# Accumulators opened earlier, and a few unused matmuls in the gaps of a routing chain

## The chip, the cores and the metric

The program runs on one core of a Trainium2 chip. The metric is the device time of one execution in microseconds, the median of the runs of each kernel. Lower is better.

## What is computed

One block of a streaming encoder for 256 tokens of width 1024, in float32. The first part is a mix of three branches; the second is a mixture of experts:

```
h = rms_norm(x); proj = h @ w_in
x = x + (gated sum of chunk attention, Mamba-2 scan, memory attention) @ w_out
# MoE on rms_norm(x):
logits = xt @ w_router + b_router            # 256 x 32
top_val, top_idx = top_k(logits, 4); wts = softmax(top_val)
for each expert e, for its tokens:
    g = min(x @ w_gate[e] + b_gate[e], 7); u = clip(x @ w_up[e] + b_up[e], -7, 7)
    y += wt * (((u + 1) * g * sigmoid(1.702 * g)) @ w_down[e] + b_down[e])
```

## The kernel before

The 256 tokens are two tiles of 128 (t = 0 and 1). Everything before the experts follows one list of steps, written out by a planner, that each engine walks in the same order. Its last block is `wo`, the product with `w_out`, in column halves i = 0 and 1. Of the last half only tile 0 stands in the list; tile 1 is done by hand, by `second_tile(0)` to `second_tile(3)`, four quarters of six matmuls each (float32r, 512 columns, L1382 to L1384).

Behind that comes the routing chain, in which TensorE, VectorE and ScalarE hand to one another. Per tile t:

- `add_out(t)` (VectorE, L1211) adds the product to the residual `x_sb`; `turn_out(t)` (TensorE transposes, L1369) and `take_xT(t)` (VectorE, L1217) make the transposed copy `xT`;
- `last_logits(t)` (TensorE, L1389, 32 columns) makes the second half of the router's logits. It needs `take_xT(t)`. VectorE finds the norm of the row meanwhile with ScalarE's help (L862 to L874);
- `choose(t)` (VectorE, L1231 to L1241) takes the logits, finds the top four and writes the 0/1 matrix `chosen_r`;
- a matmul with `upto_r` (L1620 for tile 0, L1623 and L1634 for tile 1) counts the place of each token within its expert, and `find_first(t)` (VectorE, L1248, L1250) turns it into `hot`, the selection matrix of expert 0;
- ScalarE writes the normed rows `h2` (L821), and `gather` (TensorE, L1605, 64 columns per instruction) picks the tokens of expert 0 by `hot`.

`take_gathered` (VectorE, L1262) copies the gathered tokens to `xgT`, and the loop over 32 experts begins. Expert 0 runs its gate product first (L1674). Its matmuls are of 512 columns on half of the array, 8 for each load. After the first load's 8 matmuls comes the bias (L1683), which waits for `pick` (VectorE, L1317). VectorE reaches that line only behind the tables of places and weights (L1287 to L1303) and the reading of the number of passes.

Between the logits of tile 1 and the first gather, TensorE opens the four accumulator banks `ACC` = 0 to 3 (L1627): for each one a matmul of one column of zeros with the identity, which marks the bank so that the later scatter products can add to it. They need only that `add_out(1)` has read the last product out of its bank (`gemm_taken`).

The weights of the experts come by SyncE's DMA queue (L457): six loads of 2 MB per expert into eight slots. The first eight are asked for before the loop. Each further one waits until TensorE has used its slot (`e_used`), in the order of the slots: load 8 waits for the first 8 matmuls of expert 0, load 12 for the first half of its down product (L1712).

An instruction of this program that reads float32 (not float32r) stands in the trace as two records.

Of the kernel before, what the change touches and what calls it, by code (L numbers as in the profile page):

```python
# [5 lines left out]
P = 128  # L6
# [14 lines left out]
NB = 512  # L21
# [55 lines left out]
GEMM_AT = {g: n for n, g in enumerate(GEMM)}  # L77
# [3 lines left out]
def first(name, i=0):  # L81

    return QUARTERS * BLOCK_AT[(name, i)]
# [106 lines left out]
def misc_index():  # L190

    at, n = {}, 0
    for step in SCHED:
        at[step] = n
        n += MISC_GROUPS.get(step[0], 0)
        if step[0] == "ssm":
            n += 1 + step[3]
    at["tail"] = n
    at["places"] = n + TT
    at["end"] = n + 2 * TT  # L200
    return at


MISC_AT = misc_index()
# [11 lines left out]
def hybrid_block_kernel(nc, x, mem, g_mix, w_in, w_dt, a_gains, rel_rev, conv_w, conv_b, dt_bias, a_log, d_skip,  # L216
                        g_ssm, g_mem, w_mem_kv, x_gains, w_br_a, w_br_b, w_br_c, w_out, norm_ffn, w_router,
                        b_router, w_gate, b_gate, w_up, b_up, w_down, b_down, bias_dram, out):
    with ExitStack() as ctx:
        def sb(name, shape, dt=F32):  # L220
            return ctx.enter_context(nc.sbuf_tensor(name, shape, dt))
# [3 lines left out]
        def sem(name):  # L225
            if name not in sems:
                sems[name] = ctx.enter_context(nc.semaphore(name))
            return sems[name]
# [11 lines left out]
        def placed(name, shape, dt, offset):  # L240
            return nc.alloc_sbuf_tensor_at(name, shape, dt, offset=base + 4 * offset)
# [3 lines left out]
        SR = placed("regions_r", [P, N_REGIONS, REGION], F32R, 0)  # L245
# [53 lines left out]
        ident = sb("ident", [P, P])  # L299
        upto = sb("upto", [P, P])  # L300
        after = sb("after", [P, P])
# [41 lines left out]
        upto_r = sb("upto_r", [P, P], F32R)  # L343
# [31 lines left out]
        ps = ctx.enter_context(nc.psum_tensor("ps", [P, 8, NB], F32))  # L375
        GEMM_BANKS, EXP_BANK, MISC_BANKS = (0, 1, 2, 3), 7, (4, 5, 6)
        ACC, G_BANK, U_BANK, X_BANK, D_BANK = (0, 1, 2, 3), 4, 5, 6, 7

        gemm_taken = sem("gemm_taken")
# [15 lines left out]
            return (r * LOADS + k) % SLOTS, (r * LOADS + k) // SLOTS  # L395

        MISC_END = MISC_AT["end"]
        COUNT_BANK = EXP_BANK
        GEMM_END = len(GEMM)

        def pool_rests(n):
# [3 lines left out]
        def quarter(w):  # L405

            m = w // 2
            return halves[:, m % HALVES, 2 * (w % 2):2 * (w % 2) + 2], splits[:, w % SPLITS, 0], splits[:, w % SPLITS, 1]
# [432 lines left out]
        def _(dve):  # L841
# [437 lines left out]
            dve.wait_ge(sem("counts_ready"), 1)  # L1279
            dve.tensor_reduce(cmax, ps[:, COUNT_BANK, 0:EXPERTS], AX, ALU.max).then_inc(sem("counts_taken"), 1)  # L1280
            dve.wait_ge(sem("counts_taken"), 1)
# [70 lines left out]
        def _(pe):  # L1352
            misc = [0]

            def group():

                n = misc[0]
                misc[0] += 1
                if n >= 3:
                    pe.wait_ge(misc_taken, n - 2)  # L1360
                return MISC_BANKS[n % 3]
# [6 lines left out]
            def turn(dst, src):  # L1368
                return pe.transpose(dst, src, ident[:])  # L1369
# [10 lines left out]
            def three_passes(out, lhs, rhs, start, stop):  # L1380

                pe.matmul(out, lhs[0], rhs[0], start=start, stop=False, skip_group_check=True)  # L1382
                pe.matmul(out, lhs[1], rhs[0], start=False, stop=False, skip_group_check=True)  # L1383
                return pe.matmul(out, lhs[0], rhs[1], start=False, stop=stop, skip_group_check=True)  # L1384

            def router(t, half):

                for c in range(4 * half, 4 * half + 4):
                    last = pe.matmul(ps[:, EXP_BANK, t * EXPERTS:(t + 1) * EXPERTS], xT[:, c, t * P:(t + 1) * P],  # L1389
                                     wr_sb[:, c], start=(c == 0 and t == 0), stop=(c == KC - 1), skip_group_check=True)  # L1390
                return last

            pe.wait_ge(sem("masks"), 3)
            n = 0
            for step in SCHED:
# [145 lines left out]
                elif kind == "ssm":  # L1541
                    u, g, t = step[1:]
                    if t == 1:
                        b = group()
                        pe.matmul(ps[:, b, :], cbm[:, g % 2, 2 * P:3 * P], fx[:, g * GW:(g + 1) * GW],
                                  start=True, stop=True).then_inc(misc_ready, 1)
# [3 lines left out]
                    for r in range(8):  # L1550
# [3 lines left out]
                                         start=True, stop=True)  # L1554
# [22 lines left out]
            def second_tile(q):  # L1577

                w = first("wo", 1) + q
                hi, lo = quarter(w)[1:]  # L1580
                b = GEMM_BANKS[GEMM_AT[("wo", 1, 1)] % 4]
                for c in range(2):
                    k = 2 * q + c
                    last = three_passes(ps[:, b, :], (mergedT[0][:, k, P:T], mergedT[1][:, k, P:T]),
                                        (hi[:, c], lo[:, c]), k == 0, k == KC - 1)
                last.then_inc(unit_used, 1)

            def turn_out(t):

                b = group()  # L1590
                pe.wait_ge(gemm_taken, GEMM_AT[("wo", 1, t)] + 1)
                for c in range(4):
                    last = turn(ps[:, b, c * P:(c + 1) * P], x_sb[:, t, (4 + c) * P:(5 + c) * P])
                last.then_inc(misc_ready, 1)

            def last_logits(t):

                pe.wait_ge(misc_taken, MISC_AT["tail"] + t + 1)
                router(t, 1).then_inc(sem("logits_ready"), 1)

            def gather(t0=0, t1=TT):

                for t in range(t0, t1):
                    for c in range(KC):
                        last = pe.matmul(ps[:, X_BANK, c * BLK:(c + 1) * BLK], h2[:, t, c * P:(c + 1) * P], hot[:, t],  # L1605
                                         start=(t == 0 and c == 0), stop=(t == TT - 1), skip_group_check=True)
                if t1 == TT:
                    last.then_inc(sem("gather_ready"), 1)

            second_tile(0)  # L1610
            turn_out(0)
            second_tile(1)
            last_logits(0)
            second_tile(2)
            second_tile(3)
            turn_out(1)

            b = group()
            pe.wait_ge(sem("chosen_ready"), 1)
            pe.matmul(ps[:, b, 0:EXPERTS], upto_r[:], chosen_r[:, 0], start=True, stop=True).then_inc(misc_ready, 1)  # L1620
            last_logits(1)
            b = group()
            pe.matmul(ps[:, b, 0:EXPERTS], ones_r[:], chosen_r[:, 0], start=True, stop=False, skip_group_check=True)  # L1623

            pe.wait_ge(gemm_taken, GEMM_END)
            for bank in ACC:
                pe.matmul(ps[:, bank, 0:1], ident[:], after[:, P - 1:P], start=True, stop=False, skip_group_check=True)  # L1627

            pe.wait_ge(sem("hot_ready"), 1)
            pe.wait_ge(sem("h2_ready"), 2)  # L1630
            pe.wait_ge(misc_taken, MISC_AT["places"] + 1)
            gather(0, 1)
            pe.wait_ge(sem("chosen_ready"), 2)
            pe.matmul(ps[:, b, 0:EXPERTS], upto_r[:], chosen_r[:, 1], start=False, stop=True, skip_group_check=True)\  # L1634
                .then_inc(misc_ready, 1)
            pe.wait_ge(sem("logits_taken"), TT)
            for t in range(TT):
                last = pe.matmul(ps[:, COUNT_BANK, 0:EXPERTS], ones_r[:], chosen_r[:, t], start=(t == 0), stop=(t == 1))
            last.then_inc(sem("counts_ready"), 1)
            pe.wait_ge(sem("hot_ready"), 2)  # L1640
            pe.wait_ge(sem("h2_ready"), 4)
            gather(1, 2)

            def scatter(n, signal=None):

                pe.wait_ge(sem("yb_ready"), n + 1)
                for t in range(TT):
                    for h in range(2):
                        rows = slice(64 * h, 64 * h + 64)
                        last = pe.matmul(ps[:, ACC[2 * t + h], :], hot_wT[rows, t], yb[rows], start=False, stop=False,  # L1650
                                         skip_group_check=True)
                        if signal is not None:
                            last.then_inc(signal, 1)
# [8 lines left out]
            with pe.Fori(0, n_pass) as b_:  # L1662
                with pe.Fori(0, EXPERTS // ROUND) as j_:
                    j = b_ * (EXPERTS // ROUND) + j_
                    for r in range(ROUND):
# [3 lines left out]
                        for k in range(4):  # L1669
                            bank, (slot, turns) = (G_BANK, U_BANK)[k // 2], place(r, k)  # L1670
                            pe.wait_ge(e_landed[slot], (j * TURNS + turns + 1) * 16)
                            for c in range(KC // 2):
                                for h in range(2):
                                    last = pe.matmul(ps[64 * h:64 * h + 64, bank, :], xgT[:, k % 2 * 4 + c],  # L1674
                                                     eslots[slot][:, c, h * NB:(h + 1) * NB],
                                                     start=(k % 2 == 0 and c == 0), stop=(k % 2 == 1 and c == 3),
                                                     skip_group_check=True)
                            last.then_inc(e_used[slot], 1)
                            if k % 2 == 0:

                                pe.wait_ge(sem("pick_ready"), i + 1)
                                for h in range(2):
                                    pe.matmul(ps[64 * h:64 * h + 64, bank, :], pick[0:96],  # L1683
                                              bias_parts[0:96, k // 2, h * NB:(h + 1) * NB],
                                              start=False, stop=False, skip_group_check=True)
# [17 lines left out]
                        for h in range(2):  # L1703
                            pe.matmul(ps[64 * h:64 * h + 64, D_BANK, :], pick[0:96],
                                      bias_parts[0:96, 2, h * NB:(h + 1) * NB],
                                      start=True, stop=False, skip_group_check=True)
                        for k in range(2):
                            slot, turns = place(r, 4 + k)
                            pe.wait_ge(e_landed[slot], (j * TURNS + turns + 1) * 16)
                            for c in range(4):  # L1710
                                for h in range(2):
                                    last = pe.matmul(ps[64 * h:64 * h + 64, D_BANK, :], actT[:, c, 64 * k:64 * k + 64],  # L1712
                                                     eslots[slot][:, c, h * NB:(h + 1) * NB],
                                                     start=False, stop=(k == 1 and c == 3), skip_group_check=True)
# [42 lines left out]
```

## Time and profile before

| | us |
|---|---|
| median of three runs | 1543.1 (1540.38 to 1544.27) |
| the profiled execution's own time | 1546.29 |
| its span, from first to last instruction | 1544.3 |
| TensorE busy (matmuls) | 1460.4 |
| VectorE busy | 619.2 |
| ScalarE busy | 391.3 |
| mean granted TensorE clock | 0.984 |

The profiled execution is 3.2 us longer than the median of the runs and 2.0 us longer than the longest of them. Its own time is 2.0 us more than its span. All places in it are counted in microseconds from its first instruction. The routing chain lies at about 597 to 617 us, and the loop over the experts from 617 us to 1538 us.

### The profile page before, as it was taken

How to read it: one execution, taken by the hardware profiler on the slowest of the kernel's cores; microseconds unless marked ns; L12 is line 12 of the kernel's file. 1: busy time of each engine (PE TensorE's matmuls, PEld its weight loads, DVE VectorE, ACT ScalarE, POOL GpSimd, SP SyncE). 2: the span in 40 equal slices, each digit the busy share in tenths (PEclk: the TensorE clock that was granted, in tenths of full speed). 3: DMA queues.
4: the chain of work that ended last, by engine and by line, in shares of the span. 5: the costliest groups of instructions: out<-in, count | busy, mean ns of one | idle time of the engine just before them, and what ended most of it. 6: DMA issues, size and time to landing. Idle time of an engine off the chain costs nothing.

```text
span 1544.3 us, 18679 instructions
## 1 busy us (share of the span) xinstructions
PE 1460.4 (95%) x7595; PEld 849.2 (55%) x7595; DVE 619.2 (40%) x1118; ACT 391.3 (25%) x570; POOL 151.7 (10%) x91
## 2 busy tenths in 40 slices
PE   6978997899999999999999999999999999999998
PEld 6876776777778877444444443433433433443343
DVE  5896569777775585212122221211211111112112
ACT  5435455545545443010010100100100100100010
POOL 4245322111111220000000000000000000000000
PEclk9999999999999997999999999999999999999999
DMA  7334334445444685899999999999999999999996
GB/s 243 114 132 150 104 115 136 144 154 163 144 146 177 237 323 220 334 428 427 429 428 429 429 428 428 429 429 428 428 429 429 429 428 428 429 429 428 428 429 265
DMA packets 72651, 491.39 MB, mean 318 GB/s; under 512 B 5168, under 2 KB 7344, under 8 KB 48032
## 3 DMA queue, kind: packets, MB, share of 16 engines
q1 hardware_dynamic: 69648, 487.76, 78.1%
q10 hardware_dynamic: 2448, 2.62, 0.6%
q0 software_dynamic: 512, 0.43, 0.1%
q8 instruction: 27, 0.44, 0.1%
q14 instruction: 16, 0.13, 0.0%
HBM read 489.72 MB, written 1.07 MB: 318 GB/s over the span
## 4 chain that ended last, share of the span: by engine, by line
PE 63%; DMA 23%; DVE 9%; ACT 2%; issue 2%; POOL 1%; DVEq 0%; SPq 0%; ACTq 0%
DMA regions<-in_w_up 22%; PE ps L1674 18%; PE ps L1712 10%; PE ps L1382 6%; PE ps L1383 6%; PE ps L1384 6%; PE ps L1605 5%; PE ps L1369 3%; PE ps L1650 3%; DVE splits L931 1%; DVE regions L1034 1%; DVE regions L1032 1%; ACT splits L673 1%; PE ps L1540 1%; DVE regions L950 1%
## 5 line engine op out<-in xcount | busy, mean ns | idle before, releaser
L1674 PE MATMUL ps<-regions,sig 128*64 128x512 f32 x2048 | 463.4, 597 | 25.9 <-DMA regions<-in_w_up 25.0
L1674 PEld LDWEIGHTS ps<-regions,sig 128*64 128x64 f32 x2048 | 142.1, 137 | 322.2 <-issue 263.1
L1382 PE MATMUL ps<-splits,regions_r 128*128 128x512 f32 x512 | 215.4, 421 | 11.9 <-DVE splits L931 9.2
L1712 PE MATMUL ps<-regions,tmp 128*64 128x512 f32 x1024 | 225.1, 592 | 0.0
L1383 PE MATMUL ps<-splits,regions_r 128*128 128x512 f32 x512 | 202.7, 396 | 0.0
L1384 PE MATMUL ps<-splits,regions_r 128*128 128x512 f32 x512 | 202.6, 396 | 0.0
L673 ACT ACTIVATE splits<-halves 128x1024 fp32r<-128x1024 f32 x152 | 158.7, 1054 | 107.4 <-PE ps L1384 96.9
L931 DVE TENSOR_TENSOR splits<-halves,splits 128x1024 fp32r<-128x1024 f32 x114 | 142.3, 1256 | 69.9 <-ACT splits L673 69.2
L831 ACT ACTIVATE work<-work 128x512 f32<-128x512 f32 x32 | 20.2, 630 | 528.3 <-DVE work L1327 528.3
L1712 PEld LDWEIGHTS ps<-regions,tmp 128*64 128x64 f32 x1024 | 71.9, 137 | 131.8 <-issue 129.4
L580 POOL TENSOR_TENSOR splits<-halves,splits 128x1024 fp32r<-128x1024 f32 x38 | 93.2, 2451 | 424.0 <-ACT splits L673 424.0
L1605 PE MATMUL ps<-craw,regions 128*128 128x64 f32 x1056 | 125.2, 278 | 0.1
L1605 PEld LDWEIGHTS ps<-craw,regions 128*128 128x128 f32 x1056 | 123.9, 196 | 0.3 <-DVE craw L1250 0.3
L1382 PEld LDWEIGHTS ps<-splits,regions_r 128*128 128x128 f32 x512 | 98.2, 192 | 40.5 <-DVE splits L931 11.9
L1383 PEld LDWEIGHTS ps<-splits,regions_r 128*128 128x128 f32 x512 | 98.1, 192 | 23.0 <-issue 4.1
L1384 PEld LDWEIGHTS ps<-splits,regions_r 128*128 128x128 f32 x512 | 97.9, 191 | 21.7
L1341 DVE COPY sig<-ps 128x512 f32<-128x512 f32 x32 | 22.1, 692 | 208.9 <-PE ps L1712 208.9
L1332 DVE TENSOR_SCALAR work<-ps 128x512 f32<-128x512 f32 x32 | 22.1, 692 | 193.7 <-PE ps L1674 193.7
L1327 DVE TENSOR_SCALAR work<-ps 128x512 f32<-128x512 f32 x32 | 22.1, 692 | 173.3 <-PE ps L1674 173.3
L833 ACT ACTIVATE craw<-ps 128x256 f32<-128x256 f32 x32 | 12.3, 383 | 289.7 <-PE ps L1369 289.7
L1262 DVE TENSOR_TENSOR sig<-ps,gain_rows 128x512 f32<-128x512 f32 x33 | 22.8, 691 | 144.6 <-PE ps L1605 144.6
L1650 PE MATMUL ps<-sig,craw 64*128 64x512 f32 x264 | 65.6, 615 | 0.8 <-DVE sig L1341 0.8
(243 smaller groups left out, 1346.4 us busy)
## 6 DMA issues: line engine op xcount, KB each, us to landing
regions<-in_w_gate SPq DMA_DIRECT2D x64, 2048.0 KB, 30.1
regions<-in_w_up SPq DMA_DIRECT2D x64, 2048.0 KB, 33.2
regions<-in_w_down SPq DMA_DIRECT2D x64, 2048.0 KB, 35.4
halves<-in_w_in SPq DMA_DIRECT2D x48, 1024.0 KB, 5.2
halves<-in_w_br_b SPq DMA_DIRECT2D x8, 1024.0 KB, 5.1
halves<-in_w_mem_kv SPq DMA_DIRECT2D x8, 1024.0 KB, 5.1
halves<-in_w_br_a SPq DMA_DIRECT2D x4, 1024.0 KB, 5.1
halves<-in_w_br_c SPq DMA_DIRECT2D x4, 1024.0 KB, 6.9
```

What stands on the lines that cost most here:

```text
L580: pool.tensor_tensor(lo, raw, hi.bitcast(F32), ALU.subtract).then_inc(lo_ready_pool, 1)
L673: act.activation(hi, raw, ACT.Copy).then_inc(hi_ready, 1)
L931: dve.tensor_tensor(lo, raw, hi.bitcast(F32), ALU.subtract).then_inc(lo_ready, 1)
L1262: dve.tensor_tensor(xgT, ps[:, X_BANK, :].rearrange("p (c j) -> p c j", c=KC), gain2_rows[:].unsqueeze(2).to_broadcast([P, KC, BLK]), ALU. ...
L1369: return pe.transpose(dst, src, ident[:])
L1382: pe.matmul(out, lhs[0], rhs[0], start=start, stop=False, skip_group_check=True)
L1383: pe.matmul(out, lhs[1], rhs[0], start=False, stop=False, skip_group_check=True)
L1384: return pe.matmul(out, lhs[0], rhs[1], start=False, stop=stop, skip_group_check=True)
L1605: last = pe.matmul(ps[:, X_BANK, c * BLK:(c + 1) * BLK], h2[:, t, c * P:(c + 1) * P], hot[:, t], start=(t == 0 and c == 0), stop=(t == TT ...
L1650: last = pe.matmul(ps[:, ACC[2 * t + h], :], hot_wT[rows, t], yb[rows], start=False, stop=False, skip_group_check=True)
L1674: last = pe.matmul(ps[64 * h:64 * h + 64, bank, :], xgT[:, k % 2 * 4 + c], eslots[slot][:, c, h * NB:(h + 1) * NB], start=(k % 2 == 0 and ...
L1712: last = pe.matmul(ps[64 * h:64 * h + 64, D_BANK, :], actT[:, c, 64 * k:64 * k + 64], eslots[slot][:, c, h * NB:(h + 1) * NB], start=False ...
```

## The change

Three things change, all on TensorE. The opening of the accumulators moves from behind the logits of tile 1 to ahead of them, with the wait for `gemm_taken` that goes with it. A new helper `keep_busy(bank, n)` issues n matmuls of 512 columns (float32r, operands that lie there anyway) whose result nothing reads. It is called three times: 3 matmuls ahead of `turn_out(1)`, into the bank that the first product of `wo` had; 3 behind the gather of tile 0; and 2 behind the gather of tile 1. The last two calls write to `SPARE_BANK`, the bank that held the places of tile 0.

```
-        COUNT_BANK = EXP_BANK
+        COUNT_BANK, SPARE_BANK = EXP_BANK, MISC_BANKS[MISC_AT["places"] % 3]
...
+            def keep_busy(bank, n):
+
+                for _ in range(n):
+                    pe.matmul(ps[:, bank, :], upto_r[:], SR[:, 2, 0:NB], start=True, stop=True)
...
             second_tile(3)
+            keep_busy(GEMM_BANKS[GEMM_AT[("wo", 0, 0)] % 4], 3)
             turn_out(1)
 
             b = group()
             pe.wait_ge(sem("chosen_ready"), 1)
             pe.matmul(ps[:, b, 0:EXPERTS], upto_r[:], chosen_r[:, 0], start=True, stop=True).then_inc(misc_ready, 1)
+            pe.wait_ge(gemm_taken, GEMM_END)
+            for bank in ACC:
+                pe.matmul(ps[:, bank, 0:1], ident[:], after[:, P - 1:P], start=True, stop=False, skip_group_check=True)
             last_logits(1)
             b = group()
             pe.matmul(ps[:, b, 0:EXPERTS], ones_r[:], chosen_r[:, 0], start=True, stop=False, skip_group_check=True)
-
-            pe.wait_ge(gemm_taken, GEMM_END)
-            for bank in ACC:
-                pe.matmul(ps[:, bank, 0:1], ident[:], after[:, P - 1:P], start=True, stop=False, skip_group_check=True)
...
             gather(0, 1)
+            keep_busy(SPARE_BANK, 3)
             pe.wait_ge(sem("chosen_ready"), 2)
             pe.matmul(ps[:, b, 0:EXPERTS], upto_r[:], chosen_r[:, 1], start=False, stop=True, skip_group_check=True)\
                 .then_inc(misc_ready, 1)
...
             gather(1, 2)
+            keep_busy(SPARE_BANK, 2)
```

## Rows read from the trace of the kernel before

**Rows 1.** The page: the span, and the granted clock in 40 slices (tenths).

```profile
span 1544.3 us, 18679 instructions
...
PEclk9999999999999997999999999999999999999999
```

**Rows 2.** Busy time by stretch: us; PE, PEld, DVE, ACT, POOL; clock, DMA share, GB/s.

```profile
616.00:624.00 8.00, 7.12 (x23) 2.20 (x24) 4.64 (x22) 0.00 (x0) 0.00 (x0) 0.62 0.00 0
624.00:644.00 20.00, 20.00 (x114) 9.47 (x112) 3.85 (x5) 2.89 (x4) 0.00 (x0) 1.00 1.00 410
644.00:646.00 2.00, 2.00 (x12) 0.69 (x10) 0.00 (x0) 0.00 (x0) 0.00 (x0) 1.00 0.72 197
646.00:900.00 254.00, 254.00 (x1362) 109.32 (x1360) 51.02 (x105) 26.03 (x36) 0.00 (x0) 1.00 1.01 428
```

**Rows 3.** What TensorE waited for, 900 to 1544: us in total, times, longest.

```profile
PE ps L1674 <- DMA regions<-in_w_up: 25.0, 39, 1.0
```

**Rows 4.** The chain that ended last, 601 to 630: start, us, what.

```profile
604.68 1.61 PE ps L1389 x8
...
606.48 1.69 PE ps L1627 x8
608.16 3.52 PE ps L1605 x16
...
612.39 3.69 PE ps L1605 x16
...
616.10 0.70 DVE sig L1262
...
616.94 6.20 PE ps L1674 x16
```

**Rows 5.** Busy time by stretch around the routing chain, columns as in rows 2.

```profile
602.00:605.00 3.00, 1.36 (x10) 0.90 (x8) 1.72 (x5) 0.81 (x3) 0.00 (x0) 1.00 0.73 218
605.00:608.00 3.00, 3.00 (x16) 3.00 (x16) 2.38 (x13) 1.96 (x3) 0.00 (x0) 0.51 0.97 371
...
636.00:640.00 4.00, 4.00 (x38) 3.98 (x36) 0.00 (x0) 2.26 (x3) 0.00 (x0) 1.00 0.98 418
```

**Rows 6.** TensorE in order of time: start, us, instruction, [idle before it, its releaser].

```profile
598.61 0.98 PE L1389 MATMUL ps<-wr_sb,regions 128*128 128x32 f32 x8
599.42 0.48 PE L1382 MATMUL ps<-splits,regions_r 128*128 128x512 f32 x1
...
603.27 0.63 PE L1369 MATMUL ps<-ident,regions 128*128 128x128 f32 x4 [0.87 <-DVE regions L1211]
...
604.68 1.61 PE L1389 MATMUL ps<-wr_sb,regions 128*128 128x32 f32 x8 [0.77 <-DVE regions L1217]
...
630.28 3.60 PE L1674 MATMUL ps<-regions,sig 128*64 128x512 f32 x16
...
636.44 3.68 PE L1605 MATMUL ps<-craw,regions 128*128 128x64 f32 x32
```

**Rows 7.** VectorE in order of time.

```profile
606.40 0.25 DVE L1231 SCALAR_TENSOR_TENSOR rt<-ps,stat,head_rows 128x32 f32<-128x32 f32 x1 [0.27 <-PE ps L1389]
...
611.85 0.19 DVE L1248 TENSOR_TENSOR rt<-ps,chosen_r 128x32 f32<-128x32 f32 x1 [3.65 <-PE ps L1634]
...
621.36 0.19 DVE L1317 CAST pick<-cbm 96x64 bf16 x1 [1.50 <-issue]
```

**Rows 8.** ScalarE in order of time.

```profile
606.16 2.30 ACT L821 ACTIVATE regions<-regions,stat 128x512 f32<-128x512 f32 x2 [1.04 <-DVE stat L874]
```

**Rows 9.** Other falls and returns of the clock: stretches as in rows 2, TensorE as in rows 6.

```profile
252.00:256.00 4.00, 0.77 (x4) 0.57 (x4) 3.96 (x4) 4.00 (x7) 0.14 (x1) 1.00 0.00 0
578.00:580.00 2.00, 0.19 (x2) 0.00 (x0) 2.00 (x4) 1.82 (x3) 0.00 (x0) 1.00 0.61 262
...
581.00:584.00 3.00, 3.00 (x9) 2.34 (x8) 1.91 (x3) 0.00 (x0) 0.00 (x0) 0.52 0.02 5
...
458.39 3.55 PE L1369 MATMUL ps<-ident,regions 128*128 128x128 f32 x16 [2.53 <-DVE regions L950]
```

More of the change, by code:

```diff
@@ L397, in hybrid_block_kernel @@
         MISC_END = MISC_AT["end"]
-        COUNT_BANK = EXP_BANK
+        COUNT_BANK, SPARE_BANK = EXP_BANK, MISC_BANKS[MISC_AT["places"] % 3]
         GEMM_END = len(GEMM)
@@ L1608, in gather, with keep_busy @@
                     last.then_inc(sem("gather_ready"), 1)
+            def keep_busy(bank, n):
+                for _ in range(n):
+                    pe.matmul(ps[:, bank, :], upto_r[:], SR[:, 2, 0:NB], start=True, stop=True)
             second_tile(0)
@@ L1615, in _ @@
             second_tile(3)
+            keep_busy(GEMM_BANKS[GEMM_AT[("wo", 0, 0)] % 4], 3)
             turn_out(1)
@@ L1620, in _ @@
             pe.matmul(ps[:, b, 0:EXPERTS], upto_r[:], chosen_r[:, 0], start=True, stop=True).then_inc(misc_ready, 1)
+            pe.wait_ge(gemm_taken, GEMM_END)
+            for bank in ACC:
+                pe.matmul(ps[:, bank, 0:1], ident[:], after[:, P - 1:P], start=True, stop=False, skip_group_check=True)
             last_logits(1)
@@ L1623, in _ @@
             pe.matmul(ps[:, b, 0:EXPERTS], ones_r[:], chosen_r[:, 0], start=True, stop=False, skip_group_check=True)
-            pe.wait_ge(gemm_taken, GEMM_END)
-            for bank in ACC:
-                pe.matmul(ps[:, bank, 0:1], ident[:], after[:, P - 1:P], start=True, stop=False, skip_group_check=True)
             pe.wait_ge(sem("hot_ready"), 1)
@@ L1632, in _ @@
             gather(0, 1)
+            keep_busy(SPARE_BANK, 3)
             pe.wait_ge(sem("chosen_ready"), 2)
@@ L1642, in _ @@
             gather(1, 2)
+            keep_busy(SPARE_BANK, 2)
             def scatter(n, signal=None):
```

## The prediction

> **What bounds the kernel now.** I read the page first: the span is 1544.3 us and the granted clock is full in nearly every slice, so no general slowness of TensorE is at stake [rows 1]. The stretches come next. The reader is to see that from 646 us on the DMA engines are never free (share 1.01, 428 GB/s), that TensorE has no idle time at first, and that it later waits for weights 39 times, 25.0 us in all [rows 2, 3]. The loop over the experts is thus bound by its loads, and its end moves only if the stream of loads starts earlier. It stands still from 616 to 624 us, because all eight slots are full and none is used, and it dips once more at 644 to 646 us, when load 12 waits for its slot [rows 2]. Both dips end when TensorE lets go of a slot. So whatever brings expert 0 forward brings the end forward by as much, provided it still holds at the second dip.
>
> The chain of 601 to 630 us says what expert 0 waits for: almost only TensorE's own instructions [rows 4]. The clock says why they take long. It falls at about 605 us and stays at half (0.50, which is 1.2 GHz of 2.4) until about 622 us [rows 2, 5]. What came before it fell is in the order of time: TensorE was idle 0.87 us for `add_out(1)`, then 0.77 us for `take_xT(1)` [rows 6], busy 1.36 of 3.00 us [rows 5]. At half clock the same router matmuls take 1.61 us instead of 0.98, and 16 gather records take 3.52 us, the time of 32 at full clock [rows 4, 6].
>
> **The change part by part.** Prices at full clock: the eight router records of 598.61 hold TensorE 0.81 us, until 599.42 [rows 6]. A record of 512 columns holds it 0.23 us: 16 of L1674 take 3.60 us, tail included [rows 6]. At half clock it is 0.43: 16 of them take 6.20 us, of which the last 0.9 was at full clock again [rows 2, 4]. I take the same for the unused ones. A gather of one tile is half of 3.68 us less its tail, 1.76 us.
>
> *Three unused matmuls ahead of `turn_out(1)`.* They take 3 x 0.23 = 0.69 us. They start when the last product is issued, 0.87 us before the transposes are released, so they cost nothing [rows 6]. If that cover were gone, or the clock low (3 x 0.43 = 1.3 us), they would push the transposes, `take_xT(1)` and the logits by 0 to 0.4 us.
>
> *The opening of the accumulators.* Eight records; at half clock they are 1.69 us of the chain [rows 4]. At full clock I take the router's 0.81 us, as both load a full set of weights and stream little. The trace has no such record at full clock. The bounds are a clean halving of the 1.69 us, 0.85, were it all clock, and the 1.69 us undivided, were it none; the router's pair of rows, 1.61 and 0.98, says that it is nearly all clock [rows 4, 6]. They go into the gap of 0.77 us ahead of 604.68. The wait for `gemm_taken` that moves with them holds nothing back, since the transposes ahead of it waited for the same release by `add_out(1)`. Behind it stand the logits, which could start up to 0.1 us later. That is covered, because VectorE waits for the logits only until 606.40 and its own norm is ready 0.27 us before that [rows 7].
>
> *The router and `choose(1)`.* The logits end at 604.68 + 0.81 = 605.5. VectorE's norm is then the later one, so L1231 starts at 606.15 instead of 606.40 and `chosen_r` is there at 607.9 [rows 7].
>
> *Gather of tile 0 and three more unused matmuls.* From 605.6 to 607.4, then 0.69 us to 608.1. `chosen_r` is ready at 607.9, so 0.2 us of this lies on the path. L1634, L1248 and L1250 take 0.85 us as now (611.44 to 612.3, of which 0.1 is clock) and lead to 608.95. The rows of `h2` are ready at 606.16 + 2.30 = 608.46, not later [rows 8].
>
> *Gather of tile 1.* 608.95 + 1.76 = 610.7, against 612.39 + 3.69 = 616.08 now. L1262 ends at 611.6 and L1674 starts at 611.75, against 616.94 [rows 4]: 5.2 us earlier. The last two unused matmuls (0.46 us) lie beside L1262, which takes 0.70 us.
>
> *Expert 0.* The first 16 records of L1674 take 3.45 us at full clock instead of 6.03 [rows 4, 6], another 2.6 us. That makes 7.8. But now something else is late. `pick` is written 4.76 us after the end of L1262 (616.79 to 621.55), and no part of that is TensorE's clock [rows 7]. So the bias matmuls, at 622.97 now, can start at 611.6 + 4.76 = 616.4 and not at 615.2. The gain is 7.8 - 1.2 = 6.5 us. The first slot comes free at 615.2, when the eight loads have just landed, and the stream goes on almost without a break; load 12 still finds its slot in use. The second dip moves with TensorE, by 6.5 us [rows 2].
>
> **What the sum rests on** is that the clock holds. For it: the added 0.69 us and the opening fill the two gaps, and a gather at full clock kept it at 1.00 at 636 to 640 us with no matmul of 512 columns in most of it [rows 5]. Against it: the opening streams one column per matmul and may be worth no more than idleness, and a gap alone does not decide. TensorE was busy 0.77 of 4 us at 252 us and the clock stayed at 1.00, but it fell behind the shorter gap at 578 us [rows 9]. Which places are risky depends on where the gate's moments of decision lie.
>
> The Trainium skill, "TensorE: Matmul & The Clock Gate", section "What's actually happening", says that these moments run free of the kernel and meet it elsewhere in each run. The trace agrees in so far as the two gaps above were judged differently; by that rule the second rival below holds in many executions. The same page, section "Part 4: PE-mode transpose", says that transposes do not count as activity. The trace disagrees: the clock went back to full after 458.39 to 461.7 us, in which TensorE did nothing but transposes [rows 9]. By the page the transposes at 603.27 would be another gap, and the clock would more likely fall.
>
> **Against the medians.** The sum is made against the profiled execution, 1546.29 us, and gives 1539.8. That execution is 3.2 us above the median of the runs. If the excess is the clock's (it fell later in the others), the time is that of a held clock in all, 1539.8 or somewhat less; if it is only the profiler's, it is 1543.1 - 6.5 = 1536.6. I take the middle, 1538.2.
>
> **The rivals.**
>
> 1. *The clock holds through the chain* (as summed): 1538.2, own range 1536.0 to 1540.5. Chance 0.45.
>
> 2. *The clock falls after all, a little later, at 605.6 to 607.8 us, in most executions.* The stretch from the unused matmuls' end at 602.9 holds only transposes, the opening, the logits and the start of a gather. Worked through for a fall at 605.6: gather 3.5 us to 609.1, three unused matmuls at 0.43 to 610.4, 1.0 to 611.4, gather to 614.9, L1674 from 616.0, with the clock back somewhat before its end, to 621. For one at 607.8: L1674 from 613.8, end 619.4. Against 622.97 that is 2 to 3.6 us, but an execution of the kernel before with the same late fall has part of that already. Time 1541.2, range 1539.3 to 1543. Chance 0.33.
>
> 3. *The change does not do what it says:* the clock falls at 605 as before. Then the opening at full clock in the gap saves its 1.69 us, and the second group of unused matmuls costs 3 x 0.43 = 1.3 us on the path, as `chosen_r` is long ready by then. The last group, 0.85 us, just fits beside L1262 and its hand-over. Gain 0.4 us: 1542.7, range 1541.5 to 1544. Chance 0.15.
>
> 4. *Slower.* The clock falls before the opening, which then takes 1.69 us in a gap of 0.77, and its return moves from 622 us to later, so that more of expert 0 runs at half clock. Each 16 records there cost 2.6 us more [rows 4, 6]. The opening and the unused matmuls cost 0.9 + 1.3 - 1.69 = 0.5 us net; with two groups of 16 more, 5.7 us: 1548.8. It decides from a return more than about 5 us later. Nothing in the trace holds the clock down while L1674 runs dense that long. Chance 0.07.
>
> **How the numbers follow.** A measurement of this kernel tells about 0.3%, 4.6 us, from no change. The first case passes it in about three of four ways of comparing it, the second hardly ever: faster 0.34 + 0.04 = 0.38. The third, most of the second and the rest of the first are within: 0.56. Slower 0.06. The range runs from the first case's low end, a little widened for its unknown place against the median, to the third case: 1535.5 to 1543.8.
>
> **What the profile after would show.** TensorE's granted clock at 605 to 611 us: 1.00 in case 1, a fall at 605.6 or later in case 2. L1627 between 603.7 and 604.6 with the logits still at 604.7. L1231 at about 606.15. The second gather at 609, L1262 at 611, and behind the first 16 records of L1674 an idle time of about 1.2 us that VectorE's `pick` ends, which is not there now. The DMA engines busy again by 617. The prediction is wrong if the clock holds and the end does not move, which would mean that the loads were not the bound, or if the clock falls in spite of the 0.69 us ahead of the transposes.

## The result, and the profile after

The changed kernel takes 1535.47 us (median of six executions, 1533.17 to 1538.3), the kernel before 1542.39 us (six, 1540.2 to 1549.71). The ratio is 0.995, with a 95% interval of 0.9933 to 0.9967. It is faster, and in this set by more than the 0.3% that the prediction took as the bound of measurement. The prediction was wrong by its range: 1535.47 lies 0.03 us below the low end of 1535.5, and most of its chance stood on no difference.

The page of the profile after, the lines that answer to [rows 1]:

```profile
span 1535.4 us, 18695 instructions
...
PEclk9999999999999999999999999999999999999999
```

The one weaker slice of [rows 1] is gone. Stretches of the changed kernel around the chain, columns as in [rows 2]:

```profile
597.00:600.00 3.00, 2.82 (x18) 2.17 (x16) 1.18 (x3) 1.52 (x3) 0.00 (x0) 1.00 0.88 284
600.00:603.00 3.00, 3.00 (x29) 3.00 (x28) 2.65 (x15) 1.15 (x2) 0.00 (x0) 1.00 0.83 339
603.00:606.00 3.00, 2.65 (x22) 2.42 (x20) 1.88 (x10) 2.87 (x4) 0.00 (x0) 1.00 1.03 434
...
610.00:612.00 2.00, 1.45 (x8) 0.29 (x4) 0.73 (x8) 0.00 (x0) 0.00 (x0) 1.00 0.12 49
612.00:613.00 1.00, 0.52 (x4) 0.31 (x6) 0.76 (x4) 0.00 (x0) 0.00 (x0) 1.00 0.84 164
```

The granted clock is 1.00 all through, where [rows 5] has 0.51. The loads stand still for little more than the 2 us from 610 to 612, where [rows 2] has eight. The chain that ended last, 600 to 630 us, against [rows 4]:

```profile
600.69 0.96 PE ps L1389 x8
601.65 0.10 PE ps L1632
601.75 1.83 PE ps L1605 x16
603.58 0.75 PE ps L1613 x3
...
604.38 0.20 DVE rt L1248
604.61 0.27 DVE craw L1250
...
604.92 2.01 PE ps L1605 x16
606.96 0.69 DVE sig L1262
```

In this kernel L1613 is `keep_busy`, L1629 the opening, L1681 the product of L1674 before, and L1690 its bias. TensorE in order of time:

```profile
598.13 0.86 PE L1613 MATMUL ps<-regions_r,upto_r 128*128 128x512 f32 x3
599.16 0.63 PE L1369 MATMUL ps<-ident,regions 128*128 128x128 f32 x4 [0.18 <-DVE regions L1211]
...
599.66 1.03 PE L1629 MATMUL ps<-after,ident 128*128 128x1 f32 x8
600.58 1.08 PE L1389 MATMUL ps<-wr_sb,regions 128*128 128x32 f32 x8
...
607.80 3.65 PE L1681 MATMUL ps<-regions,sig 128*64 128x512 f32 x16 [0.36 <-DVE sig L1262]
612.49 0.41 PE L1690 MATMUL ps<-bias_parts,pick 96*64 96x512 bf16 x2 [1.03 <-DVE pick L1317]
```

The wait of 0.87 us ahead of the transposes is 0.18 us of idleness now, and the wait ahead of the logits is filled by the opening. Behind the first 16 records of the gate product stands the new wait for `pick`.

The first bias matmul of the kernel before, to compare with the last line:

```profile
622.97 0.39 PE L1683 MATMUL ps<-bias_parts,pick 96*64 96x512 bf16 x2
```

From the first logits record of tile 1 to the first bias matmul of expert 0 the kernel before took 622.97 - 604.68 = 18.29 us, the changed one 612.49 - 600.58 = 11.91 us. The gain of the chain is 6.4 us.

Two other things lie between these executions. The changed kernel comes to its logits 4.1 us earlier (600.58 against 604.68), in code that is the same. And the end is only about 9 us earlier (span 1535.4 against 1544.3), though the first bias is 10.5 us earlier.

### The profile page after: what moved, and what is told of

It reads as the page before. It is cut to its first block, busy times and chain, and to the rows that moved or that the text cites. A ratio compares the mean times of both kernels' runs of the same rounds, so it can differ in the third digit from the quotient of the medians.

```text
span 1535.4 us, 18695 instructions
## 1 busy us (share of the span) xinstructions
PE 1450.0 (94%) x7603; PEld 840.8 (55%) x7603; DVE 618.8 (40%) x1118; ACT 391.0 (25%) x570; POOL 152.8 (10%) x91
## 4 chain that ended last, share of the span: by engine, by line
PE 62%; DMA 23%; DVE 9%; ACT 2%; issue 2%; POOL 1%; DVEq 0%; ACTq 0%
DMA regions<-in_w_up 22%; PE ps L1681 17%; PE ps L1719 10%; PE ps L1382 6%; PE ps L1384 6%; PE ps L1383 6%; PE ps L1605 5%; PE ps L1657 3%; PE ps L1369 3%; DVE regions L1034 2%; DVE splits L931 2%; DVE regions L1032 1%; ACT splits L673 1%; PE ps L1540 1%; DVE regions L950 1%
## 5 line engine op out<-in xcount | busy, mean ns | idle before, releaser
L1681 PE MATMUL ps<-regions,sig 128*64 128x512 f32 x2048 | 461.1, 594 | 26.4 <-DMA regions<-in_w_up 26.1
L1681 PEld LDWEIGHTS ps<-regions,sig 128*64 128x64 f32 x2048 | 141.3, 137 | 321.4 <-issue 259.7
L1382 PE MATMUL ps<-splits,regions_r 128*128 128x512 f32 x512 | 213.6, 417 | 11.8 <-DVE splits L931 9.2
L1605 PE MATMUL ps<-craw,regions 128*128 128x64 f32 x1056 | 121.8, 273 | 0.4 <-DVE craw L1250 0.4
L1605 PEld LDWEIGHTS ps<-craw,regions 128*128 128x128 f32 x1056 | 120.6, 192 | 0.5 <-DVE craw L1250 0.5
L1382 PEld LDWEIGHTS ps<-splits,regions_r 128*128 128x128 f32 x512 | 97.2, 190 | 39.9 <-DVE splits L931 11.7
L833 ACT ACTIVATE craw<-ps 128x256 f32<-128x256 f32 x32 | 12.3, 383 | 291.2 <-PE ps L1369 291.2
```

## The experiments

Each kernel was run 7 to 12 times, and the kernel before 23 to 35 times on the same chip; ratios are to it. One execution of each was profiled, so what is said of a trace is said of one execution. "The chain" is the time from the first logits record of tile 1 to the first bias matmul of expert 0, in the profiled execution.

**The parts alone.** The first four kernels each leave out a part of the change. In the first, only the opening is moved:

```diff
-            keep_busy(GEMM_BANKS[GEMM_AT[("wo", 0, 0)] % 4], 3)
...
-            keep_busy(SPARE_BANK, 3)
...
-            keep_busy(SPARE_BANK, 2)
```

> Only the opening of the accumulators is moved; there are no unused matmuls. Theory A (the change's gain is the clock, which the unused matmuls hold at full through the routing chain): the clock falls in the chain as before, so the chain from the router's last matmuls to the bias of expert 0 keeps most of its half-clock time. The gain is what the eight opening records leave of their 1.69 us on the chain plus what a later fall gives, 1.5 to 2.6 us (ratio 0.998 to 0.999). Rival B (the moved opening is what matters, and the unused matmuls are idle decoration): about the full 6.9 us of the change, ratio 0.9955.

Measured: 1538.63 us, ratio 0.9981 (0.9967 to 0.9996); chain 15.75 us (604.74 to 620.49). Stretches of its profile:

```profile
603.00:605.00 2.00, 1.68 (x16) 1.71 (x16) 1.15 (x5) 0.76 (x3) 0.00 (x0) 1.00 0.84 205
605.00:609.00 4.00, 4.00 (x24) 4.00 (x23) 2.63 (x15) 2.94 (x4) 0.00 (x0) 0.57 0.99 412
609.00:619.00 10.00, 8.98 (x32) 5.81 (x34) 4.63 (x23) 2.33 (x3) 0.00 (x0) 0.50 0.52 220
```

The clock falls at 605.5 and comes back at 619.2 us. The gain of the chain is 2.5 us, within what theory A gave. Rival B, which wanted a ratio of about 0.9955, is out: it lies below the interval.

The second kernel keeps the unused matmuls, with the opening at its old place:

```diff
-            pe.wait_ge(gemm_taken, GEMM_END)
-            for bank in ACC:
-                pe.matmul(ps[:, bank, 0:1], ident[:], after[:, P - 1:P], start=True, stop=False, skip_group_check=True)
             last_logits(1)
             b = group()
             pe.matmul(ps[:, b, 0:EXPERTS], ones_r[:], chosen_r[:, 0], start=True, stop=False, skip_group_check=True)
+            pe.wait_ge(gemm_taken, GEMM_END)
+            for bank in ACC:
+                pe.matmul(ps[:, bank, 0:1], ident[:], after[:, P - 1:P], start=True, stop=False, skip_group_check=True)
```

> The three calls of unused matmuls stay, the opening of the accumulators is back behind the logits. Theory A: the clock holds past 605 us in most executions, but the opening is 0.85 us more on the path at full clock and is one more thin stretch, so the clock may fall at about 608 us: gain 0.6 to 5.8 us. If the clock holds throughout, the loss against the whole change is 0.85 us less the time in which the places of tile 0 are waited for anyway, so a ratio of 0.996 to 0.9965. Rival B: ratio 1.000 or above.

Measured: 1539.46 us, ratio 0.9991 (0.9976 to 1.0006), no difference that can be told, and less than theory A had for a clock that holds; chain 15.70 us (599.07 to 614.77), in the part of the expectation in which the clock falls after all. In its trace the fall has moved to 603.1, 4.0 us behind its first logits record (599.07), where before it was 0.4 us behind:

```profile
599.00:603.00 4.00, 3.94 (x34) 3.94 (x35) 2.93 (x18) 2.64 (x4) 0.00 (x0) 1.00 1.00 414
603.00:606.00 3.00, 2.85 (x12) 2.50 (x12) 1.11 (x6) 1.38 (x2) 0.00 (x0) 0.52 1.00 423
```

The first group of unused matmuls gets the clock past the first danger, and with the opening on the path behind the logits there is a second one. The opening does two things there: it is thin work itself, and it puts the second group later (3.70 us behind the first logits record, against 2.81 in the changed kernel). Which of the two counts is not shown.

The third keeps the moved opening and the first group only:

```diff
             gather(0, 1)
-            keep_busy(SPARE_BANK, 3)
...
             gather(1, 2)
-            keep_busy(SPARE_BANK, 2)
```

> The opening is moved and only the three unused matmuls ahead of the transposes of tile 1 stay. Theory A with all three groups needed: the clock gets past 605 us but falls between the two gathers or behind them, at about 608 us; gain 2 to 3.5 us (ratio 0.998). If the first group alone holds the clock, the gain is that of the whole change plus the 0.2 us that the second group lies on the path, ratio 0.9955, and the later two groups do nothing. Rival B: as the whole change.

Measured: 1537.61 us, ratio 0.9979 (0.9962 to 0.9996); chain 14.98 us (604.25 to 619.23). The clock falls at 608.5 us, 4.2 us behind the first logits record (604.25):

```profile
604.00:608.00 4.00, 3.74 (x32) 3.53 (x31) 3.28 (x19) 2.47 (x3) 0.00 (x0) 1.00 0.96 397
608.00:612.00 4.00, 3.65 (x17) 3.44 (x16) 0.91 (x6) 2.82 (x4) 0.00 (x0) 0.56 1.03 436
```

In the changed kernel the second group runs from 2.8 us behind the first logits record and the third from 6.2 us behind it. At this fall only the second is missing. Whether the third is needed too was not tried.

The fourth has the later two groups only:

```diff
             second_tile(3)
-            keep_busy(GEMM_BANKS[GEMM_AT[("wo", 0, 0)] % 4], 3)
             turn_out(1)
```

> The opening is moved and the unused matmuls behind the gathers stay (3 and 2); the three ahead of the transposes of tile 1 are gone. Theory A: the clock falls at about 605 us as before, the three in the chain then run at half clock, 1.3 us, and the gain is 1.5 us (ratio 0.999) or somewhat more if they bring the clock back earlier. If instead it is the groups behind the gathers that count, the gain is near the whole change's 6.9 us.

Measured: 1538.55 us, ratio 0.9987 (0.9971 to 1.0002); chain 16.41 us (599.02 to 615.43). The clock falls at 599.75, 0.7 us behind the first logits record, and the three unused matmuls stand in the chain at half clock:

```profile
600.48 3.49 PE ps L1605 x16
603.98 1.39 PE ps L1613 x3
```

So none of these four parts has the effect of the whole. Each of the four loses the clock somewhere in the chain, and their gains in the chain are 2.5, 2.6, 3.3 and 1.9 us, against 6.4 for all together.

**More executions of the changed kernel**, the same program twice more, each time beside the runs that follow here:

> The changed kernel itself once more, on the chip of the runs that follow, for more executions. If the clock holds through the chain in every execution (theory A, strong form), the granted clock of all executions is 0.991 or more, as in the six there are, and the ratio is 0.995 to 0.996. If the gate's moments decide (rival C: the clock holds only where they lie well, in about half of the executions), some executions show a clock near 0.988 and take 3 to 5 us longer, and the ratio comes out at 0.997 to 0.998.

> The changed kernel a third time, as the reference on this chip: ratio 0.9955 to 0.997, about a third of the executions with a granted clock of 0.991 or less and 2 to 5 us more.

Measured: 1536.22 us, ratio 0.9966 (0.9953 to 0.9979), and 1536.9 us, ratio 0.9972 (0.9959 to 0.9986). The chain is 11.92 (599.63 to 611.55) and 11.91 us (598.74 to 610.65) in the two profiles, with a clock of 1.00 in it. Neither form of the first expectation came: 0.9966 lies between its 0.995 to 0.996 and its 0.997 to 0.998, and executions with 0.989 and 0.990 are among the eleven. The second ratio is just above what was expected. Over the three sets the mean of 26 executions is 1536.5 us; that of the 85 of the kernel before on the later chips is 1541.8, a difference of 5.3 us or 0.34%. Ten of the 26 show a mean granted clock of 0.991 or less, and I had taken that beforehand for a sign of a fall in the chain. The run with filled gaps, below, shows that a clock of 0.990 is none.

**Unused matmuls that stream little.** The same eight instructions, with 32 columns:

```diff
-                    pe.matmul(ps[:, bank, :], upto_r[:], SR[:, 2, 0:NB], start=True, stop=True)
+                    pe.matmul(ps[:, bank, 0:32], upto_r[:], SR[:, 2, 0:32], start=True, stop=True)
```

> The unused matmuls stay where they are, eight in number, but stream 32 columns instead of 512. Theory A (what counts is the work they give TensorE to stream): as with the moved opening alone, ratio 0.998, the clock falls in the chain, and the chain from the first logits record of tile 1 to the bias of expert 0 takes about 15.5 us. Rival D (it is enough that instructions are issued in the gaps): ratio as for the whole change, chain 11.9 us.

Measured: 1539.63 us, ratio 0.9993 (0.9981 to 1.0006); chain 16.07 us (600.23 to 616.30), where 0.998 and 15.5 us were expected. The clock falls at 601.0 us, 0.7 us behind the first logits record:

```profile
600.00:603.00 3.00, 3.00 (x20) 3.00 (x20) 2.62 (x16) 1.49 (x3) 0.00 (x0) 0.66 0.96 404
603.00:607.00 4.00, 3.85 (x19) 3.75 (x19) 1.39 (x8) 2.51 (x3) 0.00 (x0) 0.50 0.99 420
```

So it is not the presence of instructions that holds the clock; rival D is out. The thin matmuls also fill less time: ahead of the transposes they leave 0.63 us of idleness, where those of 512 columns leave 0.18. How much is streamed and how long TensorE is held are not told apart by this run.

**Twice as many:**

```diff
-            keep_busy(GEMM_BANKS[GEMM_AT[("wo", 0, 0)] % 4], 3)
+            keep_busy(GEMM_BANKS[GEMM_AT[("wo", 0, 0)] % 4], 6)
...
-            keep_busy(SPARE_BANK, 3)
+            keep_busy(SPARE_BANK, 6)
...
-            keep_busy(SPARE_BANK, 2)
+            keep_busy(SPARE_BANK, 4)
```

> Each group of unused matmuls is doubled (6, 6 and 4 of 512 columns). By the costs of the prediction: the first six take 1.38 us in a gap of 0.87, so the transposes start 0.5 us later; the second six are 0.7 us more on the path; the last four, 0.92 us, reach just past the hand-over through VectorE. So 1.2 us slower than the changed kernel where the clock holds in both. If the single groups hold the clock only sometimes (rival C), the doubled ones hold it more often, and the median could come out equal or faster by 0.5 us.

Measured: 1535.96 us, ratio 0.9971 (0.9958 to 0.9983), against 0.9966 for the changed kernel beside it, which the medians can't tell apart. Its trace tells more:

```profile
597.40 1.55 PE L1613 MATMUL ps<-regions_r,upto_r 128*128 128x512 f32 x6
598.79 0.60 PE L1369 MATMUL ps<-ident,regions 128*128 128x128 f32 x4
...
602.99 1.64 PE L1613 MATMUL ps<-regions_r,upto_r 128*128 128x512 f32 x6
...
607.02 1.18 PE L1613 MATMUL ps<-regions_r,upto_r 128*128 128x512 f32 x4
```

The transposes now follow the first six without idleness: the cover is used up. From the last product's last record to the logits it takes 0.3 us more than in the changed kernel, and the chain is 12.60 us, 0.7 us longer. That makes 1.0 us where I expected 1.2. The medians do not show it at the end.

**The wait for `pick` behind other work.** In the gate and up products of every expert, the bias goes ahead of the last quarter of the second load's matmuls. It is meant for expert 0, the only one that waits for `pick`:

```diff
                             for c in range(KC // 2):
+                                if k % 2 == 1 and c == 3:
+                                    pe.wait_ge(sem("pick_ready"), i + 1)
+                                    for h in range(2):
+                                        pe.matmul(ps[64 * h:64 * h + 64, bank, :], pick[0:96],
+                                                  bias_parts[0:96, k // 2, h * NB:(h + 1) * NB],
+                                                  start=False, stop=False, skip_group_check=True)
...
-                            if k % 2 == 0:
-
-                                pe.wait_ge(sem("pick_ready"), i + 1)
-                                for h in range(2):
-                                    pe.matmul(ps[64 * h:64 * h + 64, bank, :], pick[0:96],
-                                              bias_parts[0:96, k // 2, h * NB:(h + 1) * NB],
-                                              start=False, stop=False, skip_group_check=True)
```

> The changed kernel, with the two bias matmuls of the gate and up products issued ahead of the last quarter of the second load's matmuls instead of behind the first load's. The wait for pick, 1.03 us of TensorE idle in the profile after, lies then beside 6 us of other matmuls in expert 0. Expert 0 and all that follows come 1.0 us earlier, loads and end too: ratio to the changed kernel 0.9993. Rival: the loads have become the bound and the end does not move.

Measured: 1536.42 us, ratio 0.9965 (0.995 to 0.998), the same as the changed kernel beside it. In its trace the wait is gone:

```profile
607.14 6.23 PE L1687 MATMUL ps<-regions,sig 128*64 128x512 f32 x28 [0.35 <-DVE sig L1262]
613.20 0.39 PE L1683 MATMUL ps<-bias_parts,pick 96*64 96x512 bf16 x2
```

`pick` of expert 1 is written 635.65 - 599.93 = 35.7 us behind the first logits record, against 637.52 - 600.58 = 36.9 us in the changed kernel. The 1.2 us is shown at expert 1. That it reaches the end is not shown by these medians, whose interval is 2.3 us to either side. In the one trace it seems to: the span is 1544.3 - 1532.5 = 11.8 us shorter than before, of which 604.68 - 599.93 = 4.75 us lie ahead of the logits, so 7.1 us are left. The same subtraction gives 4.9, 5.1 and 6.4 us for the three traces of the changed kernel.

**The thinnest stretch filled.** The changed kernel with two more ahead of the opening, and then this together with the late bias:

```diff
+            keep_busy(GEMM_BANKS[GEMM_AT[("wo", 0, 0)] % 4], 2)
             for bank in ACC:
```

> The changed kernel with two more unused matmuls of 512 columns, ahead of the opening of the accumulators. They fill the thinnest stretch of the chain (transposes, opening, logits). They delay the logits of tile 1 by 0.4 us, which VectorE's norm covers (it is ready 0.6 us after the logits' end at full clock). Rival C (the clock holds in the changed kernel only where the gate's moments lie well, and fell in 5 of 17 executions so far): with the stretch filled it holds in all or nearly all, the median is 0.5 to 1.5 us below the changed kernel's, ratio 0.9955 to 0.996 to the kernel before, and no execution shows a clock of 0.990 or less. If the falls of those executions lie elsewhere in the kernel, nothing changes: the same share of low clocks, or the extra 0.2 to 0.4 us on the path.

> The same two more unused matmuls and the bias of the gate and up products behind other matmuls of expert 0. Another 1.1 us earlier than the run before it, as the late bias alone gave in its trace: ratio 0.995 to 0.9955 to the kernel before, the fastest of all. If the loads are the bound, no gain over the run before it.

Measured: 1536.45 us, ratio 0.9966 (0.9951 to 0.998), and 1535.79 us, ratio 0.9962 (0.9947 to 0.9978), beside 0.9972 of the changed kernel. The second has the lowest median on its chip, but the intervals overlap almost wholly, and both ratios missed what was expected, by 0.0006 and 0.0007. Nor did low clocks vanish: the first has one execution of nine at 0.990, the second four of twelve at 0.990 or below.

The first of the two is worth more for its trace. This execution happens to meet the clock at the same places as the profiled one of the kernel before: it falls at 52.09, 93.05, 127.18, 147.66, 263.71, 308.09, 458.27 and 581.15 us, as that one did to within 0.01 us. It comes to its logits at 604.88 instead of 604.68 us. The stretches that answer to [rows 9] and [rows 5]:

```profile
581.00:584.00 3.00, 3.00 (x9) 2.29 (x9) 1.61 (x2) 0.00 (x0) 0.00 (x0) 0.53 0.02 5
...
605.00:608.00 3.00, 3.00 (x28) 2.96 (x28) 2.36 (x14) 2.09 (x2) 0.00 (x0) 1.00 0.98 421
```

and TensorE in order of time, where L1682 and L1691 are the gate product and its bias:

```profile
604.88 1.06 PE L1389 MATMUL ps<-wr_sb,regions 128*128 128x32 f32 x8
...
612.08 3.65 PE L1682 MATMUL ps<-regions,sig 128*64 128x512 f32 x16 [0.35 <-DVE sig L1262]
616.76 0.41 PE L1691 MATMUL ps<-bias_parts,pick 96*64 96x512 bf16 x2 [1.03 <-DVE pick L1317]
```

Up to the logits the two executions differ by 0.2 us, so what is behind is the chain's. The bias comes 622.97 - 616.76 = 6.2 us earlier, and the span is 1544.3 - 1538.2 = 6.1 us shorter. Expert 0's head start goes through the whole loop, to the end. And this execution has a mean clock of 0.990 with no fall in the chain: eight falls ahead of it are enough. So a mean clock of 0.990 is no sign that the chain lost it, and what I had taken as evidence for rival C is none. In none of the seven traces with the moved opening and all the groups at 512 columns (three of the changed kernel, four of its variants) did the clock fall in the chain. That is not all executions: two with the late bias have 0.988, and two with filled gaps and late bias 0.987 and 0.988, which is more half clock than these eight falls make. Where it lay no trace shows, so that the chain loses the clock now and then is not excluded.

## Why the prediction was wrong, and where it was right

**What bounds the kernel: right.** The start of the stream of loads sets the end, in the main. In the pair just compared 6.2 us at expert 0 became 6.1 us at the end; in the changed kernel's first trace 10.5 us became 9.0 (below).

**The sum of the chain: right.** Counted from the first logits record, forecast against the changed kernel: second gather at 4.3 us against 604.92 - 600.58 = 4.3; L1674 at 7.1 against 7.2; bias at 11.7 against 11.9. The forecast gain was 6.5 us, the measured one 6.4. The wait for `pick` was forecast at 1.2 us and is 1.03. The opening at full clock holds TensorE 0.92 us and not 0.81, and ends just as the logits are released. The unused matmuls behind the first gather lie 0.3 us on the path, where I had 0.2: VectorE's L1241 ended at 603.80 and L1640 started at 604.17, 0.37 us later, while without them the same hand-over takes 0.05 us (607.46 to 607.51, with the first group alone). The first group, the later two together and the moved opening turned out each to be needed, which the prediction had not worked out one by one.

**Against the medians: this step failed.** The sum made 1539.8 us from the profiled execution and 1536.6 from the median of the runs, and I took the middle, 1538.2. The reason was that the profiled execution's 3.2 us above the median might be clock time of this very chain, which would then be gained only once. So half of the excess, 1.6 us, was put on top of 1536.6. The runs show none of it in the chain, and the gain there was whole, 6.4 us. The traces in which the clock fell unaided have the fall at 0.4, 0.8, 0.7 and 0.7 us behind the first logits record (before, moved opening alone, late groups, thin), so nearly the whole half-clock time lies in the chain of each. The extra time of the profiled execution comes from falls ahead of the chain: 604.68 us against 598.7 to 601.2 for the logits in nine of the twelve later traces. The filled kernel's trace has the same falls ahead and none in the chain, and its execution is also 3.6 us above its median (1540.06 against 1536.45). So the gain should have been taken from the median whole: 1536.6.

**Luck on both sides.** The three sets of the changed kernel have 1535.47, 1536.22 and 1536.9, around 1536.6. But the medians of the kernel before were lower than the 1543.1 that I started from: 1542.39, 1541.54 and 1540.91. The gains of the sets are thus 6.9, 5.3 and 4.0 us, and over all executions 5.3, less than the 6.4 of the chain and not far from the 4.9 that the middle had given, for a wrong reason. In the three traces of the changed kernel the part of the gain that is left at the end is 4.9, 5.1 and 6.4 us; what two of them lose lies in the loop. How long the chain is in the other executions of the kernel before, no trace shows.

**The range: also too tight at its low end.** Executions of the same kernel lie 5 us (changed, first set) to 11 us (before, 35 executions) apart. A low end only 1.1 us below 1536.6, for a median of a few of them, left no room for that. The later two sets lie inside the range, so that the first came out 0.03 us below it is chance.

**The second rival: wrong, and it took the chance from the first.** It said that the gate's moments meet the chain elsewhere in each execution, so that the clock falls later in most. The Trainium skill ("TensorE: Matmul & The Clock Gate", section "What's actually happening") has the moments run free of the kernel. The traces agree for the first part of the kernel, where the first fall is at 52 or 53 us in some executions and at 74 or 75 in others. They do not agree for the chain: unaided, the fall came 0.4 to 0.8 us behind the first logits record in all four traces. What ties the chain to the gate is not shown. In all thirteen traces there is a fall at 575.5 to 581.7 us, 23.1 to 23.8 us ahead of the logits. The four unaided falls stand 23.9 us behind that one, and the two that the first group put off (opening at its old place, and first group alone) 27.3 us. That earlier fall may be what ties them; no run was made to test it. What the rival priced for a later fall, 2 to 3.6 us, is what those two runs gained in the chain: 2.6 and 3.3.

**The third and fourth rivals** did not come about. The costs that they rest on are real, as the kernel with the late groups alone shows (1.39 us for three unused matmuls at half clock, forecast 1.3), but even it came out at 0.9987.

**What stays open.** In the profiled execution of the changed kernel 1.5 us of the 10.5 us of the chain and the alignment are lost in the loop. The writes of `pick` for experts 12 and 13 show where TensorE feels it, first in the kernel before, then in the changed one:

```profile
951.83 0.18 DVE L1317 CAST pick<-cbm 96x64 bf16 x1
979.92 0.18 DVE L1317 CAST pick<-cbm 96x64 bf16 x1
...
941.57 0.18 DVE L1317 CAST pick<-cbm 96x64 bf16 x1
970.94 0.18 DVE L1317 CAST pick<-cbm 96x64 bf16 x1
```

The lead is 10.5 us for experts 1 to 11 and 9.0 us from expert 13 on. Up to there an expert takes 27.6 us and TensorE sets the pace; behind it an expert takes 29.4 us and the loads do. The loads had lost the time long before: of each load's 16 parts the last lands 10.5 us earlier for those loads that the kernel before had in at 654 to 663 us, and 9.1 us earlier for those from 712 us on. In the second trace of the changed kernel the lead goes from 11.4 to 10.2 us in the same way, in the third (12.3 to 12.4) and in the filled kernel (6.2 to 6.1) it hardly changes. Why some executions lose it was not tried.

## What to carry to other kernels

Where TensorE waits on other engines in short turns ahead of a long stage, look at the granted clock of that stretch and of what follows: here two waits of 0.9 and 0.8 us were followed by 17 us at half clock, and 6.4 us of 18.3 came back for an opening moved and eight matmuls whose result nothing reads. Such filler must be thick enough (512 columns did it, 32 did not), must fit the waits, and must go on along the chain: the first group alone put the fall off from 0.8 to 4.2 us behind the first logits record, and no further. Compare executions that meet the same falls elsewhere, or many executions, because the alignment of the rest of the kernel is worth as much as the change.

## What the runs showed that I had not expected

The spread of one unchanged kernel follows its mean granted clock. Of 85 executions of the kernel before, the 11 with a clock of 0.985 took 1545.4 us on the mean, the 24 with 0.987 took 1541.2, and the 11 with 0.989 took 1538.9. The change as a whole moves the mean by 5.3 us, less than that spread.
